# Finishing two output chunks one token tile at a time in a seven-stage transformer kernel

## The reference, cut to what matters

```python
h = modulate(rms_norm(x, norm_g[layer, 0]), sh1, sc1)
y = gmlp_mixer(...) or nsa_mixer(...)          # one per layer
x = x + g1[:, None, :] * rms_norm(y, norm_g[layer, 1])
h = modulate(rms_norm(x, norm_g[layer, 2]), sh2, sc2)
y = jnp.square(jax.nn.relu(h @ ff_w_in[layer])) @ ff_w_out[layer]
x = x + g2[:, None, :] * rms_norm(y, norm_g[layer, 3])
...
x = x + gt1 * rmsnorm(yx @ w_out[i], g_post_mix[i])     # second block, gated linear attention
hx = modulate_2(rmsnorm(x, g_pre_ffn[i]), sh2, sc2)
x = x + gt2 * rmsnorm(conv_ffn(hx, ...), g_post_ffn[i])
```

## Time and profile before

| | |
|---|---|
| three runs | 1096.52, 1098.85, 1099.38 us |
| median | 1098.85 us |
| the profiled execution | 1101.1 us, span 1099.4 us from first to last instruction |
| mean granted TensorE clock | 0.992 of full speed |
| PE, DVE, ACT, POOL busy | 1056.8, 792.7, 531.3, 47.4 us |
| HBM read | 239.30 MB, 219 GB/s over the span |

### The profile page before, as it was taken

One profiled execution on the slowest core, in us unless ns is written; L12 is line 12 of the kernel. 1 busy time (PEld: TensorE's weight loads), 2 busy tenths in 40 slices (PEclk: granted clock), 3 DMA queues, 4 the chain that ended last, 5 costly groups with the idle time before them and its releaser, 6 DMA issues.

```text
span 1099.4 us, 17637 instructions
## 1 busy us (share of the span) xinstructions
PE 1056.8 (96%) x7288; PEld 915.3 (83%) x7300; DVE 792.7 (72%) x1171; ACT 531.3 (48%) x694; POOL 47.4 (4%) x77
## 2 busy tenths in 40 slices
PE   5899999999999999999999999999998989999997
PEld 2786799889888999877888798789997679999995
DVE  1458598768868988837855679681489469878796
ACT  2442554335356457746453334542744365444443
POOL 0000000000000000000000000030163000000000
PEclk9999999999999999999999999999899999999999
DMA  9996779887983994022957799714333356564510
GB/s 361 375 373 233 275 269 354 324 318 277 332 278 120 316 386 143 2 74 73 390 190 269 269 368 399 247 42 139 128 116 97 111 177 206 181 216 164 192 39 39
DMA packets 129787, 243.59 MB, mean 222 GB/s; under 512 B 6360, under 2 KB 101163, under 8 KB 122539
## 3 DMA queue, kind: packets, MB, share of 16 engines
q1 hardware_dynamic: 125200, 238.77, 61.4%
q10 hardware_dynamic: 4507, 3.69, 1.2%
HBM read 239.30 MB, written 1.05 MB: 219 GB/s over the span
## 4 chain that ended last, share of the span: by engine, by line
PE 79%; DVE 11%; DMA 3%; ACT 3%; issue 2%; SPq 2%; DVEq 0%; ACTq 0%
PE bank L1780 24%; PE bank L1705 12%; PE bank L1707 11%; PE bank L1706 11%; DMA raw<-in_ada_w_dram 2%; PE bank L1628 2%; DVE wlo L1035 2%; SPq L550 2%; PE bank L1674 2%; ACT whi L616 1%; PE bank L1717 1%; PE bank L1718 1%; PE bank L1719 1%; PE bank L1983 1%; DMA raw<-in_b_w_in_dram 1%
## 5 line engine op out<-in xcount | busy, mean ns | idle before, releaser
L1035 DVE TENSOR_TENSOR wlo<-raw,whi 128x2048 fp32r<-128x2048 f32 x145 | 329.3, 2276 | 122.5 <-ACT whi L616 121.5
L616 ACT ACTIVATE whi<-raw 128x2048 fp32r<-128x2048 f32 x145 | 274.9, 1897 | 173.3 <-PE bank L1780 52.5
L1705 PE MATMUL bank<-hcat,whi 128*128 128x256 f32 x1096 | 314.3, 287 | 1.2 <-DVE wlo L1035 1.2
L1706 PE MATMUL bank<-hcat,whi 128*128 128x256 f32 x1096 | 311.0, 284 | 0.0
L1707 PE MATMUL bank<-hcat,wlo 128*128 128x256 f32 x1096 | 311.0, 284 | 0.0
L1705 PEld LDWEIGHTS bank<-hcat,whi 128*128 128x128 f32 x1096 | 211.2, 193 | 11.4 <-issue 7.7
L1706 PEld LDWEIGHTS bank<-hcat,whi 128*128 128x128 f32 x1096 | 211.2, 193 | 1.3
L1707 PEld LDWEIGHTS bank<-hcat,wlo 128*128 128x128 f32 x1096 | 211.2, 193 | 0.0
L1586 DVE SCALAR_TENSOR_TENSOR cvt<-ut,vec,cvt 128x189 f32<-128x189 f32 (+2 forms) x176 | 68.2, 430 | 22.7 <-ACT cvt L1002 20.2
L1780 PE MATMUL bank<-whi,fhi 128*128 128x512 f32 x240 | 77.6, 404 | 0.0
L1780 PE MATMUL bank<-wlo,fhi 128*128 128x512 f32 x240 | 75.5, 396 | 0.0
(11 more groups left out here) (393 smaller groups left out, 1725.3 us busy)
## 6 DMA issues: line engine op xcount, KB each, us to landing
raw<-in_ada_w_dram SPq DMA_DIRECT2D x48, 1024.0 KB, 7.7
raw<-in_ff_w_in_dram SPq DMA_DIRECT2D x32, 1024.0 KB, 8.1
raw<-in_ff_w_out_dram SPq DMA_DIRECT2D x32, 1024.0 KB, 7.3
raw<-in_w_ada_dram SPq DMA_DIRECT2D x24, 1024.0 KB, 9.0
raw<-in_w_up_dram SPq DMA_DIRECT2D x22, 1024.0 KB, 5.2
raw<-in_w_in_dram SPq DMA_DIRECT2D x12, 1024.0 KB, 8.0
raw<-in_w_down_dram SPq DMA_DIRECT2D x11, 1024.0 KB, 5.0
raw<-in_a_w_in_dram SPq DMA_DIRECT2D x8, 1024.0 KB, 12.5
```

The lines of the kernel that those rows point to most:

```text
L616: act.activation(whi[:, m % SPL, 0:w], raw[:, pl.nm[m] % RAW, 0:w], ACT.Copy).then_inc(s_hi, 1)
L1035: dve.tensor_tensor(wlo[:, m % SPL, 0:w], raw[:, pl.nm[m] % RAW, 0:w], whi[:, m % SPL, 0:w], ALU.subtract).then_inc(s_lo, 1)
L1705: pe.matmul(dst, wh[:, kt, n], ah[:, kt, :], start=kt == 0, stop=False)
L1706: pe.matmul(dst, wh[:, kt, n], al[:, kt, :], start=False, stop=False)
```

## The change

Six edits:

1. The last two output chunks of gmlp, ffn0, attn, ffn1 and gla are multiplied in the order: last-but-one chunk for tile 0, last chunk for tile 0, last-but-one for tile 1, last for tile 1 (`end_of_y`). Two hooks stand between: `between` (a wait or gain rows) and `then` (the `ada_cols` of the modulation, at boundaries 1 to 4).
2. `boundary` is now: transposes of tile 0, 16 dummy matmuls (`WARM_BOUNDARY`), transposes of tile 1. `update_x` and the squares run tile 0 to its end, with `xd`, before tile 1. The high split of the next stage's second chunk moves between the y squares and the x squares of tile 1.
3. `open_y` is gone; the first chunk starts its banks itself.
4. In attn the gain's diagonal is made ahead of the last two `low` steps. In gmlp and gla one more high split is made ahead of the gain rows.
5. The four chunks of modulation G2B are multiplied at boundary 5 in the place of its dummies, and its `ada_cols` follows the first product of ffn2.
6. POOL makes its masks right after the first product of ffn1. Only the two rows of ones wait for ffn1's end.

```diff
-WARM_BOUNDARY, WARM_START = 22, 3
+WARM_BOUNDARY, WARM_START = 16, 3
...
+            def end_of_stage(u, m):
+
+                y_squares(u, m, 0)
+                x_squares(u, 0)
+                y_squares(u, m, 1)
+                splits(m + 3)
+                x_squares(u, 1)
...
-                splits(M_WO[3] + 1)
+                splits(M_WO[3] + 2)
                 gain_row(U_GLA, 0)
                 gain_row(U_GLA, 1)
+                end_of_stage(U_GLA, M_WO[3])
+
+            if has("ffn2"):
+                modulate(7, A_N11, S2B, (s_xT, 20))
                 ada_row(G2B)
...
+                for tt in range(2):
+                    half_of_y(tt)
+                    times_gain(2 * tt)
+                    times_gain(2 * tt + 1)
+                    norm_of_y(tt)
+                    add(2 * tt)
+                    add(2 * tt + 1)
+                    if e is not None:
+                        half_of_x(e, tt)
+                        norm_tile(e, tt)
+                    if not tt and between is not None:
+                        mods(between)
...
+                dve.wait_ge(s_osum, NPAIR)
+                gain_diag(U_ATT, G_N5)
                 low(NPAIR - 2)
                 low(NPAIR - 1)
-                dve.wait_ge(s_oh, 8)
-                gain_diag(U_ATT, G_N5)
...
+            def dummies(e):
 
                 pe.wait_ge(s_gain, 2 * e)
                 keep_warm(WARM_BOUNDARY, 6)
-                x_transposes(e)
+
+            def boundary(e, meanwhile=dummies):
+
+                x_transposes(e, 0)
+                meanwhile(e)
+                x_transposes(e, 1)
...
+            def end_of_y(m, r0, r1, between, then):
+
+                split_ready(m)
+                tile_onto_y(m, *r0, 0)
+                between()
+                split_ready(m + 1)
+                last_tile_onto_y(m + 1, *r1, 0)
+                then()
+                tile_onto_y(m, *r0, 1).then_inc(s_mm, 1)
+                last_tile_onto_y(m + 1, *r1, 1).then_inc(s_mm, 1)
...
+                def squares_ready():
+                    pe.wait_ge(s_fact, c0 + 16)
+                    ada_sum(ends_at(f, 14))
+
+                r14 = squares(14)
+                at_ = lambda b: (lambda k, s: b[:, 15 % 3, T * k + s.start:T * k + s.stop])
+                end_of_y(m0 + 30, r14, (at_(fhi), at_(flo)), squares_ready, lambda: ada_cols(ends_at(f, 14)))
...
+                end_of_y(M_BO[2], h_rows(4), h_rows(6), last_heads, lambda: ada_cols(S1B))
...
+                end_of_y(M_WO[2], h_rows(2 * WO_ORDER[2]), h_rows(2 * WO_ORDER[3]), gains, lambda: None)
 
             if has("ffn2"):
-                boundary(5)
+                def last_modulation(e):
+
+                    pe.wait_ge(s_l4, 2)
+                    pe.wait_ge(s_msr, 2)
+                    ada_chunks(4)
+
+                boundary(5, last_modulation)
...
                 up(M_UP[0], 6, o=7)
+                ada_cols(G2B)
                 up(M_GA[0], 4)
-                open_y()
...
+                pool.wait_ge(s_mm, M_FF[1] + 32)
+                pool.wait_ge(s_gm3, 3)
+                for n, a in enumerate((alx, alc)):
+                    pool.memset(a[32:33, :], 1.0).then_inc(s_al1, 1)
+                    pool.wait_ge(s_al1, n + 1)
```

More of the change, by code:

```diff
@@ L647, in use_roots, with y_squares @@
                 act.activation(dull[:, :], eps[:, :], ACT.Sqrt)
-            def y_squares(u, m):
-                for i in range(4):
+            def y_squares(u, m, tt):
+                for i in (2 * tt, 2 * tt + 1):
                     if i < 3:
@@ L655, in y_squares, with x_squares @@
                         act.wait_ge(s_mm, m + 1)
[L656 to L663, removed]
+                    act.activation(junk[i], ps[i][:, :], ACT.Square, accum_out=ssy[:, tt, i % 2:i % 2 + 1]).then_inc(s_sqy, 1)
+                act.wait_ge(s_sqy, 4 * u + 2 * tt + 2)
+                root_of(ssy, tt)
+            def x_squares(u, tt):
+                for i in (2 * tt, 2 * tt + 1):
                     if u < 0:
@@ L1140, in add @@
                                              op0=ALU.mult, op1=ALU.add).then_inc(s_x, 1)
[L1142 to L1160, removed]
-                if later is not None:
-                    mods(later)
+                for tt in range(2):
+                    half_of_y(tt)
[9 more added lines that the diff above has]
+                        mods(between)
             def split_h(o, dh, dl):
@@ new lines, in tile_onto_y @@
+            def tile_onto_y(m, ah, al, t, first=False):
+                wh, wl = w_of(m, 2)
+                s, n = slice(P * t, P * t + P), [slice(0, 512), slice(512, 1024)]
+                for k in range(2):
+                    a, b = ah(k, s), al(k, s)
+                    for i, (st_, w) in enumerate(((a, wh), (a, wl), (b, wh))):
+                        for half in range(2):
+                            mm = pe.matmul(ps[2 * t + half][:, :], st_, w[:, k, n[half]], start=first and k + i == 0, stop=False,
+                                           skip_group_check=True)
+                return mm
@@ new lines, in last_tile_onto_y @@
+            def last_tile_onto_y(m, ah, al, t):
+                wh, wl = w_of(m, 2)
+                s = slice(P * t, P * t + P)
+                for half in range(2):
+                    n = slice(512 * half, 512 * half + 512)
+                    for k in range(2):
+                        for st_, w in ((ah(k, s), wh), (ah(k, s), wl), (al(k, s), wh)):
+                            mm = pe.matmul(ps[2 * t + half][:, :], st_, w[:, k, n], start=False, stop=False, skip_group_check=True)
+                    if t + half < 2:
+                        mm.then_inc(s_yb, 1)
+                return mm
@@ new lines, in rows_onto_y, with last_rows_onto_y @@
+            def rows_onto_y(m, ah, al, first=False):
+                split_ready(m)
+                for t in range(2):
+                    mm = tile_onto_y(m, ah, al, t, first)
+                mm.then_inc(s_mm, 1)
+            def last_rows_onto_y(m, ah, al):
+                split_ready(m)
+                for t in range(2):
+                    mm = last_tile_onto_y(m, ah, al, t)
+                mm.then_inc(s_mm, 1)
+            def end_of_y(m, r0, r1, between, then):
+                split_ready(m)
+                tile_onto_y(m, *r0, 0)
[5 more added lines that the diff above has]
+                last_tile_onto_y(m + 1, *r1, 1).then_inc(s_mm, 1)
@@ L1887, in _ @@
                 pe.wait_ge(s_wTc, 2)
-                open_y()
                 ada_chunks(2)
-                for j in range(4):
+                for j in range(3):
                     pe.wait_ge(s_oa, j + 1)
@@ L1893, in _ @@
                         mix(3)
+                    if j < 2:
+                        rows_onto_y(M_AO[j], *h_rows(2 * j), first=j == 0)
+                        ada_chunks(2)
                     if j == 2:
@@ L2040, in _ @@
                         pe.wait_ge(s_Sev, NH)
-                        open_y()
-                        rows_onto_y(M_BO[0], *h_rows(0)).then_inc(s_mm, 1)
+                        rows_onto_y(M_BO[0], *h_rows(0), first=True)
                     turn(2 * p + 1)
```

178 lines of the change are left out of this document (61 added, 117 removed).

## The result

The changed kernel takes 1080.49 us, median of 4 runs (1079.37 to 1081.72), against 1097.68 us (1095.81 to 1099.38) for the kernel before: ratio 0.9844, 95% interval 0.9821 to 0.9867, so 17.2 us less. The forecast was 1084.2 us, 14.6 us less, with a range of 1079.5 to 1090. The profiled execution has a span of 1079.4 us.

The account below looks back on a forecast made before the run. PE holds 79% of the chain, so the gain lies in its waits, dummies and needless work, chiefly at five boundaries. The terms sum to 14.6 us, taking the median of 1098.85 to 1084.2 us, range 1079.5 to 1090.

Parts of the forecast that it names:

- boundaries 1, 2, 3, 4, columns counted: Last output matmul to first product: shorter stretches, less 0.9 us for `ada_cols` at 1, 2, 4; gains 0.7, 0.8, 2.3, 0.8.
- boundary 5, stretch: Between gla and ffn2: the last modulation's matmuls replace the dummies, and the stretch falls from 13.8 to 8.0 us, gaining 5.8.
- zeros in ffn0, ffn1, ffn2: Ahead of the first output chunk: dropping `open_y`'s four zero matmuls gains 0.4, 0.4 and 0.9 us.
- zeros and diagonal in attn: In attn: dropping the zero matmuls gains 0.8 us, and making the gain's diagonal earlier removes a PE wait of 1.2.
- masks in ffn1: Start of ffn1: POOL's selects hold up a busy DVE; cost between 0 and 10 us, taken as 2.5.
- The waits in the hooks: Feed-forward stages: last squares needed after one half-chunk, 2.8 us; a few tenths if it bites, taken as nothing.
- The step-by-step sum for tile 1's own chain: At the boundaries: 5.9 us from tile 1's last matmul to its diagonal, plus 1.77 to the first product, 7.7 us.
- tile 0's chain ends about when PE finishes tile 1: At the boundaries: tile 0's 5.9 us chain is covered by tile 1's 24 matmuls, 5.5 us.
- at 23.55 of 24 DVE can't win it back there: Start of ffn1: DVE, busy 23.55 of 24 us, can't recover time lost to POOL's selects; priced at 2.5 us.
- The overlapped gain: Rival: tile 0's chain, a load or a split is late at the boundaries; 5.4 us given back, about 1090; chance 0.13.
- The clock rival: Rival: the clock falls to 1.2 GHz behind idle time, 7.9 us at each of five boundaries, 1123; chance 0.03.
- The moved edit does nothing: Rival: all five boundaries keep their stretch while `ada_cols` costs 0.9 three times; 1.5 us left, 1097; chance 0.03.

Follow-up runs that it names:

- the chunks whole: Changed kernel with its tile order alone undone: both tiles of the last chunk but one, then both of the last, chain split by tiles; 1095.93 us, ratio 0.9984.
- the chain joint: Changed kernel keeping the matmul order, but with both tiles' norm chain interleaved on DVE and all transposes behind 22 dummies; 1093.23 us, ratio 0.9952.
- the kernel with the masks back: Changed kernel with POOL's masks back behind the last matmul of ffn1; 1084.78 us, ratio 0.9875.
- before, again: The kernel before the change, unchanged, run and profiled once more; 1098.82 us, ratio 1.0001.
- no dummies: Changed kernel without dummy matmuls at boundaries 1 to 4; 1084.54 us, ratio 0.987.
- the one with dummies among the gates: Changed kernel with `ada_cols` moved behind tile 0's transposes at boundaries 1 to 4, 12 boundary dummies, plus six among gla's gate matmuls; 1078.7 us, ratio 0.9812.

## Why the prediction was right, and where not

Term by term, in us gained. Measured values are differences of stretches between the two traces unless an experiment is named, with the falls of the clock taken out.

| term | predicted | measured |
|---|---|---|
| boundaries 1, 2, 3, 4, columns counted | 0.7, 0.8, 2.3, 0.8 | 0.8, 0.9, 2.5, 1.2 |
| boundary 5, stretch | 5.8 | 4.5 (6.2 with the fall of the clock) |
| third chunk of gla earlier | 2.4 | 2.5 |
| its columns behind the first product | -0.75 | -0.4 |
| zeros in ffn0, ffn1, ffn2 | 0.4, 0.4, 0.9 | 0.4, 0.4, 0.9 |
| zeros and diagonal in attn | 0.8 + 1.2 | 1.4 to 2.2 |
| masks away from gla's first product | 1.4 | 1.6 |
| masks in ffn1 | -2.5 | 0.0 |
| sum | 14.6 | 16.7 to 17.5 |

The measured time lies 3.7 us below the forecast. Of that 1.2 us is the kernel before, which came out at 1097.68 and not at the 1098.85 that the forecast starts from; the rest is the gain, 17.2 in place of 14.6. That the sum is so near is in part luck: the masks were priced 2.5 us too high and the gain at boundary 5 1.3 us too high, and the two errors partly cancel. The waits in the hooks, put at nothing, were nothing: ffn0 took 192.48 us against 191.91, and 0.57 is the columns' 0.95 less the zeros' 0.4.

- *Edits 1 and 2.* The step-by-step sum for tile 1's own chain gave 7.7 us, and 7.5 came out; the second group of transposes waited 0.42 us, where 0.5 was forecast. The run with the chunks whole shows that the chain's order alone gives nothing at these boundaries; the one with the chain joint, that the matmul order alone gives 0.9 us of 1.8 at best. The prediction had said that tile 0's chain ends about when PE finishes tile 1; this is the condition, and with the chunks whole it fails by 2 us and the stretch is back at 9.75.
- *Boundary 5.* The stretch came out at 7.6 us where 8.0 was forecast, but the cause was wrong. The prediction put the whole 5.8 us under edit 5. Putting the modulation back leaves 7.57 us there: edits 1 and 2, with edit 4's early high split, cured the boundary. And 1.6 of the 13.8 us were a fall of the clock that the same program didn't have in its second profile: 12.14 us, with the same 2.97 us of idle time but transposes of 3.84 us at full clock.

```profile
893.30 3.84 PE L1674 MATMUL bank<-xd,x 128*128 128x128 f32 x32 [2.97 <-DVE xd L1108]
```

- *Masks in ffn1.* This is the term that was mis-sized, by 2.5 us. The step that failed was "at 23.55 of 24 DVE can't win it back there". DVE did lose: its two low splits from 537.63 took 5.07 us where the kernel with the masks back needs 4.71, and they start 1.55 us later behind the first product, 1.9 us in all. But PE had more lead than that: in the whole of ffn1 it waited for a low split once, 0.23 us, and 0.2 us with the masks back too, where 2.5 us of such waits were forecast. And DVE got the 1.9 us back at once, out of its next wait (order of time, the kernel with the masks back and then the changed kernel):

```profile
542.72 0.69 DVE L1283 TENSOR_TENSOR fhi<-fr 128x512 fp32r<-128x512 f32 x1 [3.55 <-ACT fr L742]
```
```profile
544.34 0.69 DVE L1283 TENSOR_TENSOR fhi<-fr 128x512 fp32r<-128x512 f32 x1 [1.65 <-ACT fr L742]
```

  A busy share in a stretch tells nothing of the lead at its start. And most of the price fell on the other side (order of time of the changed kernel; the selects' median before was 0.65 us):

```profile
537.63 5.07 DVE L1035 TENSOR_TENSOR wlo<-raw,whi 128x2048 fp32r<-128x2048 f32 x2
...
538.06 3.36 POOL L2313 TENSOR_SCALAR_AFFINE_SELECT lmask<-lmask 128x128 int8<-128x128 int8 x1
```

  The select of 3.36 us begins behind the first of the two low splits and ends at 541.42, within the second. The 14 selects of the level masks took 22.0 us here and 10.1 us in the kernel before, so POOL paid 11.9 us and DVE 1.9. The Trainium skill, SBUF — State Buffer, section "Who interferes with whom", says that the instruction issued first holds the shared ports and the other one blocks. The trace agrees: both engines were held up, and with DVE back to back it was mostly POOL. The prediction read from that rule only what DVE would lose.
- *Attn.* By the whole stage the two terms were worth 1.4 us and not 2.0, seen in two executions without a fall of the clock in attn: 500.73 - 338.87 = 161.86 us (before, again) and 497.93 - 337.47 = 160.46 us (masks put back). But the wait for a low split in the middle of attn differs between executions, as said above. From its end to the last output matmul it takes 107.42 us in the first, and 105.84, 105.60 and 105.21 us in the three of the changed attn that have no fall there (masks put back, chunks whole, no dummies). That is 1.6 to 2.2 us, so the forecast of 2.0 may well be right. The diagonal's wait, 1.20 us in before, again, is gone in all of them; the zeros get the 0.4 to 1.0 that is left.
- *The clock in gla.* The first two profiles differ by 6.8 us in gla, of which 1.6 + 2.5 = 4.1 are the edits; 3.0 are falls of the clock behind the gate matmuls less 0.3 elsewhere. The second profile of before has a fall of 1.5 us there and one of 1.5 us later. Seven of the twelve profiles with the change or parts of it, the one with dummies among the gates included, had none at the gates, and neither of the two of before was without. That is too few to say that the change makes them rarer. Some of it may be in the medians, whose difference of 17.2 us has an interval of 14.6 to 19.6; the terms' sum lies well inside.
- *Rivals.* The overlapped gain didn't come: tile 0's chain ended in time at the first four boundaries and 0.22 us late at the fifth, and no load or split was late in ffn2. The clock rival needed the dummies gone. "The moved edit does nothing" is about what the kernels with one order alone show, at 0.9984 and 0.9952.

## What to carry to other kernels

Where two tiles go through one serial chain on in-order engines, bring the first to its end early (the producer's order) and let the chain finish it before the second (the consumers' order). Do both: with one of them undone, 12 to 15 of the 17 us were gone here, though in the chain-joint run 1.34 us at a boundary is the placing of a high split. Then put whatever work is owed anyway between the two tiles' transposes, and not ahead of the last tile. And before a step is priced by the busy share of an engine, ask how far ahead of its consumer that engine is, and where its next wait lies.

## What the hardware did that I had not expected

- One program shows different falls of the granted clock from execution to execution, at full PE occupancy too: 18.29 and 15.26 us for the same matmuls of gla, with a granted clock of 0.59 and 0.56 in the one and 1.00 in the other. A second profile of both kernels is worth more than a fine reading of the first.
- An idle time of 2.97 us ahead of the transposes of boundary 5 went with half clock in one execution of before and with full clock in the other. 2.94 us with the chunks whole and 2.56 us with the chain joint both went with half clock. Idle times of 3.96 us went with it at four boundaries of four, one of 1.60 us (boundary 3 of before) didn't.
- Where POOL's 14 selects met a DVE that issued back to back, DVE lost 1.9 us and POOL 11.9.
